# High and low parts of the experts' stationary tiles interleaved element by element

## What is computed

```python
def moe_swiglu(x, router, w1, w3, w2):
    logits = (xt @ router).astype(F32)
    top_v, top_i = lax.top_k(logits, TOP_K)
    gates = jax.nn.softmax(top_v, axis=-1)
    combine = jnp.sum(jax.nn.one_hot(top_i, N_EXPERTS, dtype=F32) * gates[..., None], axis=1)
    for e in range(N_EXPERTS):
        out = out + combine[:, e:e + 1] * swiglu(xt, w1[e], w3[e], w2[e]).astype(F32)
```

## Time and profile before

| | |
|---|---|
| median of three runs | 1505.19 us |
| the profiled execution, its own time | 1508.43 us |
| its span, first to last instruction | 1506.6 us |
| TensorE matmul busy | 1479.1 us, 98% |
| TensorE weight load busy | 1297.6 us, 86% |
| VectorE busy | 1236.9 us, 82% |
| ScalarE busy | 962.0 us, 64% |
| mean granted TensorE clock | 0.995 |

### The profile page before, as it was taken

How to read it: one execution, slowest core, us unless ns; L and a number is a source line. 1 busy time by engine, 2 the same in 40 slices (tenths; PEclk the granted TensorE clock), 3 DMA queues, 4 the chain that set the end, 5 groups by cost and what they waited for, 6 DMA issues and landing times.

```text
span 1506.6 us, 23455 instructions
## 1 busy us (share of the span) xinstructions
PE 1479.1 (98%) x8803; PEld 1297.6 (86%) x8804; DVE 1236.9 (82%) x906; ACT 962.0 (64%) x693; POOL 83.8 (6%) x65
## 2 busy tenths in 40 slices
PE   9998999999999999999999999999999999999997
PEld 8987899999999978888888888888888888888885
DVE  6898866656578779889888888888888888988987
ACT  6644353333353567777777777777777777777774
POOL 1035200000000030000000000000000000000300
PEclk9999999999999999999999999999999999999998
DMA  8745697888654669999999999999999999999990
GB/s 311 225 131 157 221 342 267 305 297 300 228 182 168 228 227 413 403 367 389 376 381 382 373 393 375 377 385 376 382 392 359 387 395 361 388 385 364 407 413 36
DMA packets 212938, 483.97 MB, mean 321 GB/s; under 512 B 8810, under 2 KB 26314, under 8 KB 209820
## 3 DMA queue, kind: packets, MB, share of 16 engines
q1 hardware_dynamic: 209224, 473.67, 85.2%
q10 hardware_dynamic: 2388, 5.32, 1.0%
q0 software_dynamic: 1280, 4.33, 0.7%
HBM read 446.45 MB, written 36.87 MB: 321 GB/s over the span
## 4 chain that ended last, share of the span: by engine, by line
PE 86%; DVE 1%; issue 0%; ACT 0%; DVEq 0%
PE Q L2544 20%; PE Q L2495 14%; PE Q L2497 14%; PE Q L2496 14%; PE Q L2039 7%; PE Q L2040 7%; PE Q L2041 7%; PE Q L2528 2%; DVE wlo L1174 1%; PE Q L2474 0%; PE Q L2505 0%; ACT yrows L1149 0%; PE Q L2400 0%; PE Q L2408 0%; PE Q L2032 0%
## 5 line engine op out<-in xcount | busy, mean ns | idle before, releaser
L1174 DVE TENSOR_TENSOR wlo<-raw,whi 128x2048 fp32r<-128x2048 f32 x413 | 940.3, 2297 | 186.2 <-ACT whi L988 109.3
L988 ACT ACTIVATE whi<-raw 128x2048 fp32r<-128x2048 f32 x336 | 642.2, 1919 | 169.8 <-PE Q L2497 81.1
L2495 PE MATMUL Q<-whi,xgh 128*128 128x512 f32 x896 | 354.2, 395 | 0.0
L2497 PE MATMUL Q<-whi,xgl 128*128 128x512 f32 x896 | 349.6, 390 | 0.0
L2496 PE MATMUL Q<-wlo,xgh 128*128 128x512 f32 x896 | 348.9, 389 | 0.0
L2039 PE MATMUL Q<-xh,whi 128*128 128x264 f32 x1024 | 294.7, 288 | 5.4 <-DVEq L1285 1.8
L2040 PE MATMUL Q<-xl,whi 128*128 128x264 f32 x1024 | 292.0, 285 | 0.0
L2041 PE MATMUL Q<-xh,wlo 128*128 128x264 f32 x1024 | 290.7, 284 | 0.0
L2039 PEld LDWEIGHTS Q<-xh,whi 128*128 128x128 f32 x1024 | 193.8, 189 | 8.1 <-issue 4.1
L2497 PEld LDWEIGHTS Q<-whi,xgl 128*128 128x128 f32 x896 | 168.1, 188 | 35.8
L2496 PEld LDWEIGHTS Q<-wlo,xgh 128*128 128x128 f32 x896 | 168.5, 188 | 33.6
(11 more groups left out here) (286 smaller groups left out, 1138.8 us busy)
## 6 DMA issues: line engine op xcount, KB each, us to landing
raw<-in_moe_w SPq DMA_DIRECT2D x336, 1024.0 KB, 7.1
raw<-in_ffn_w SPq DMA_DIRECT2D x42, 1024.0 KB, 7.3
raw<-in_hgrn_w_in SPq DMA_DIRECT2D x16, 1024.0 KB, 7.3
xg_rows<-zeros SPq DMA_DIRECT2D x6, 2048.0 KB, 10.9
y_rows<-zeros SPq DMA_DIRECT2D x6, 2048.0 KB, 11.7
raw<-in_conv_w_in SPq DMA_DIRECT2D x12, 1024.0 KB, 5.4
raw<-in_hgrn_w_out SPq DMA_DIRECT2D x4, 1024.0 KB, 5.0
raw<-in_conv_w_out SPq DMA_DIRECT2D x4, 1024.0 KB, 5.1
```

Of the source, the lines that this page charges most:

```text
L988: a.activation(bufs(q)[0], raw[:, n % RAW, PW * (q % 2):PW * (q % 2 + 1)], ACT.Copy).then_inc(hi_done, 1)
L1174: v.tensor_tensor(low, raw[:, slot, PW * half:PW * (half + 1)], high.bitcast(F32), ALU.subtract).then_inc(lo_done, 1)
L2495: t_.matmul(out, xgh[:, kt, :], high[:, w], start=(kt == 0), stop=False)
L2497: mm = t_.matmul(out, xgl[:, kt, :], high[:, w], start=False, stop=(kt == DT - 1))
```

## The change

The four tiles become two, `xgp` [128, 8, 128, 2] and `htp` [128, 4, 128, 2]. The last axis holds the high part at 0 and the low part at 1; the old names are views of them, so that an element of `xgh` has one of `xgl` behind it and the next of `xgh` 8 bytes on. The same holds for the last block's copies. Total sizes are the same, and the tiles around them keep their places (`LIFT` is 0). No instruction is added, removed or put elsewhere: on every engine the order is the one before, with `xgp` and `htp` in the place of the old names.

```diff
+        LIFT = 0
...
-        (xs, xgh, xgl, xg, hs, hx, hth, htl), o = region(
-            R0, ("xs", [P, TT, D], F32), ("xgh", [P, DT, P], F32R), ("xgl", [P, DT, P], F32R),
+        (xs,), o = region(R0, ("xs", [P, TT, D], F32))
+        (xgp, xg, hs, hx, htp), o = region(
+            o + LIFT, ("xgp", [P, DT, P, 2], F32R),
             ("xg", [P, D], F32), ("hs", [P, FW], F32), ("hx", [P, FW], F32),
-            ("hth", [P, 4, P], F32R), ("htl", [P, 4, P], F32R))
+            ("htp", [P, 4, P, 2], F32R))
+        xgh, xgl, hth, htl = xgp[:, :, :, 0], xgp[:, :, :, 1], htp[:, :, :, 0], htp[:, :, :, 1]
...
-        (hth_last,), _ = region(xgh_at, ("hth_last", [P, 4, P], F32R))
-        (htl_last,), _ = region(xgh_at + size([P, DT, P], F32R), ("htl_last", [P, 4, P], F32R))
+        (htp_last,), _ = region(xgh_at, ("htp_last", [P, 4, P, 2], F32R))
+        hth_last, htl_last = htp_last[:, :, :, 0], htp_last[:, :, :, 1]
```

## The result

The changed kernel takes 1530.68 us (median of 6 runs, 1530.43 to 1533.76) against 1505.88 of the kernel before in the same session: ratio 1.0168, 95% interval 1.0156 to 1.0181. That is 25 us slower. The forecast was no change with a range up to 1524; the time lies outside it. Rival 1 had the direction and the mechanism's outline, and a price that was too low (+18 us).

The account below looks back on a forecast made before the run. TensorE, busy 98% of the span, was taken to bound the kernel, with loads hidden in a 227 ns pitch. Terms of 0 on TensorE and 0 on the others left 1505.2 us, no change; range 1502.5 to 1524.

Parts of the forecast that it names:

- Rival 1: Expert stage: strided load disturbs the matmul stream, pitch above 227 ns; +18 us, 1523 us, chance 0.22.
- rival 2: Expert stage: strided load doubles and shows 63 times, after the transposes of a turn; +6.7 us, 1511.9 us, chance 0.16.
- rival 5: Expert stage: loads don't overlap matmuls of the same rows; with doubled loads 427 us, 1932 us, a chance of nothing.
- 108 ns: Time a 128-column load holds its path, from three steps between the transposes of `turn`; leaves 119 ns of 227 slack.
- (b): ScalarE's 65 writes of xgh and hth, now at 8-byte steps: taken as 0, at worst +1.4 us together with VectorE's.
- (c): VectorE's 65 writes of xgl and htl, also reading the high part: taken as 0, at worst +1.4 us together with ScalarE's.
- the bound of doubling: Upper end for ScalarE's 0.59 us copy and VectorE's 0.68 us subtraction when strided; even doubled taken as covered.
- the load disturbing the matmul: Expert stage: strided load holding up the moving stream, both read from SBUF at once; taken as 0 from the `pick` rows.
- The 3.6 ns of the earlier trace: 264-column stage: pitch 120.5 ns against 116.9 scaled from 227; as a disturbance over 4032 matmuls, 14.5 us.
- The 5.5 ns of the earlier trace: Nine matmuls right after a turn: pitch 232 ns instead of 227; as a disturbance over 4032 matmuls, 22.2 us.
- the load's own 0: TensorE's strided loads of the four tiles: no longer, since rate depends on column count and two hits a line suffice; 0.
- Rival 3: After turns: the disturbance of nine matmuls by 5.5 ns goes away, 56 times; 2.8 us faster, 1502.4 us, chance 0.07.

Follow-up runs that it names:

- run 5: Kernel computing nothing of the reference: stationary tiles of 1 to 128 columns, packed or 8-byte step, operands moved singly or together; packed 128 columns 226.7 ns, one column 231.2.
- Run 1: Kernel computing nothing of the reference, one property changed per block of 48 matmuls, such as stride or tile offset; packed 226.7 ns, step 2 233.3, packed moved 64 bytes 233.3.
- run 3: Kernel computing nothing of the reference: stationary tile's base moved by 0 to 240 bytes, plus load rates by element step; packed at 0 226.7 ns, at most other places about 233.
- experiments 2 and 6: As fast as before: changed kernel with high and low parts as alternating packed 512-byte rows, 1.0001; kernel before with pieces and stationary tiles both moved 64 bytes, 1.0003.

## Why the prediction was wrong

**What held.** The stage is bound by TensorE's pitch and by nothing else; every change of time in these runs is, to within 3 us, a change of the steady pitch times 4032 matmuls (the rows alone: 2688, the hidden columns alone: 1344). The load is hidden behind a 512-column matmul, did not double (rival 2), and overlaps matmuls of the same rows (rival 5). Its 108 ns are 110 by the prediction's own three steps of 0.33 us, which changes nothing. (b) and (c) cost nothing: ScalarE 45 ns more on a copy, inside the bound of doubling, VectorE 1 ns, and from 564.5 to 1463 us TensorE never waits.

**The step that failed** is the last term, "the load disturbing the matmul", taken as 0 because of the earlier trace rows: the same 227 ns with 8 columns loaded as with 128, hence "in the steady state a load takes nothing from the stream". The row was read as a case with almost no load. Two of its three loads are full ones, and run 5 shows that a load's effect does not follow its size: one column costs 231.2, eight columns 226.7, eight and 128 in turn 227.5, and the very pattern of the row, 8, 128 and 128, at other places 235.4. So the row showed that its own setting runs at 227, not that loads take nothing. The comparison that was wanted was between places, and the kernel before has only one in that stage: all its stationary tiles and pieces begin on multiples of 256 bytes. What the change met in place of the assumed 0 is 6.6 ns a matmul: 233.3 ns for the interleaved tiles, against 226.7 for packed ones at that place. No block of 512 columns ran faster than 226.5 ns, so whether a part of the 227 is a disturbance too stays open.

**Its size.** Rival 1 priced it from two rows at 3.6 to 5.5 ns, 14.5 to 22.2 us, and the range reached 1524. Neither row measures this. The 3.6 ns of the earlier trace rows came of scaling 227 ns by the columns, as if all of it grew with them. Run 1's 264-column block with everything on multiples of 256 bytes has 120.0 ns, so the 120.5 of the kernel hold half a nanosecond of disturbance at most. The 5.5 ns of the earlier trace rows, 4.2 over all turns, belong to tiles that are packed and stand where they stand in the steady stretches, so they have another cause. Whole groups of 24 matmuls in the stage average, before and after: 226.9 and 233.6 ns on the rows, 226.7 and 233.7 on the hidden columns, 232.0 and 237.3 behind a turn, where the first, exposed step went from 316 to 323 ns and the next nine rose by 2.8 only. That is 1344 x (6.7 + 7.1 + 5.3) = 25.7 us, against 25.3 measured (23.5 to 27.3 by the interval).

**The reason for the load's own 0** was half right. The Trainium skill ("SBUF — State Buffer", the note on cachelines under "Door 1: The DMA port swizzle") has two hits in a 16-byte line at full bandwidth. By this trace step 2 lengthens the load from 188 to 195 ns and its rate at 128 columns from 110.6 to 117.9 ns, so it is nearly but not quite free, and a step of 4, which leaves one element to such a line, doubles the load (227 against 109.6 ns, run 3); but the stream beside a step-2 load pays about as much again, which the rule doesn't cover. Where it differs the measurement stands.

**What stays open.** The runs show that the pitch of a 512-column fp32r stream depends on the difference of the two operands' places, with 256 bytes giving the same as 0, and on the load's step and length. They don't show what in SBUF or TensorE makes it so, why so many different settings come to 233.3, or why a load of 64 columns is better off at step 2 than packed. Place and step don't fix the pitch alone either, as the nine matmuls behind a turn show in the kernel before. Rival 3 (that disturbance goes away) came true in an unforeseen sense: in the changed kernel nothing is left of it on average, but because the steady pitch rose above it. In the kernels of experiments 2 and 6 that are as fast as before, the nine still have 230.5 and 230.2 ns.

## What to carry to other kernels

In a stream of long fp32r matmuls with hidden weight loads, keep both operands on the same offset modulo 256 bytes and a full stationary tile packed; a 64-byte gap in front of the stationary tiles cost 1.6% of this kernel, about as much as the interleaving did (1.7%), the same gap in front of the pieces 0.5%. Before taking a pitch for a floor, move one operand by 64 bytes and look at it again: a row from a single layout can't show what layout costs. High and low parts can share a tile if each of them keeps whole packed rows.

## What the runs showed of the hardware that was not expected

- The pitch of packed 512-column matmuls is 226.7 ns at offsets 0 and 256 bytes, 230.8 at 8, 233.3 at 16 and at 64.
- Beside its columns a matmul of 384 takes about 13 ns: 173.5 ns for 160 ns at the granted 2.4 GHz; 512 columns 226.7 for 213.3, the same 13 ns, and so 256 and 320 columns (119.8 and 146.7). 448 and 480 columns, at the same places, take 16 to 17 ns (202.7 and 216.7), 264 columns 10 (120.0). Step 2 costs at most 0.6 ns with 256, 320, 384, 448 or 480 columns, 3.3 with 264 and 6.6 with 512.
- The moving operand doesn't stand a step of 2 at all: (384.94 - 363.30) / 48 = 451 ns, twice the packed 226.7, at the full clock. The stationary one at step 2 costs 3%.
- A load of one column disturbs the stream more than a packed one of 128 at the good place, 231.2 against 226.7 ns.
- A load of 128 columns at a step of 4 elements is recorded as 310 ns, longer than the pitch of its stream, and still that stream slows only to 235 ns (run 1).
